# Attention stage of a two-layer trunk: the low parts of the weights of keys, values and queries on GpSimd, and taps 12 to 21 of the last two convolution chunks ahead of the blocks' additions

## Time and profile before

| | us |
|---|---|
| three runs | 1467.14, 1471.12, 1465.32 (median 1467.14) |
| profiled execution | 1472.86 |
| its span, first to last instruction | 1471.1 |
| PE busy | 1447.4 (98%) |
| VectorE busy | 1188.1 (81%) |
| ScalarE busy | 932.8 (63%) |
| GpSimd busy | 60.4 (4%), 70 instructions |
| line 990 (the taps), VectorE | 103.6, 240 instructions |
| line 961 (low parts of dense and expert weights), VectorE | 843.7, 369 instructions of 2.29 |

### The profile page before, as it was taken

The page is one execution under the profiler, slowest core; times in us unless marked ns, Lnnn a source line. Parts: engine busy times, 40 slices in busy tenths (PEclk is TensorE's granted clock), DMA queues, the critical chain, the costliest instruction groups (busy, mean ns, idle before and its releaser), DMA issues.

```text
span 1471.1 us, 18960 instructions
## 1 busy us (share of the span) xinstructions
PE 1447.4 (98%) x7380; PEld 1189.1 (81%) x7380; DVE 1188.1 (81%) x1109; ACT 932.8 (63%) x878; POOL 60.4 (4%) x70
## 2 busy tenths in 40 slices
PE   7999999999999999999999999999999999999998
PEld 6864999998765888888888888888888888888886
DVE  5995545447995788988898898888889888889887
ACT  4273343434373777777777777777777777777774
POOL 1042000000141000000000000000000000000000
PEclk9999999999999899999999999999999999999999
DMA  7750755532822799999999999999999999999993
GB/s 245 231 170 34 253 188 185 172 115 89 278 94 82 274 363 375 369 363 354 339 364 369 376 351 365 370 336 364 369 369 363 356 371 330 365 376 364 367 368 132
DMA packets 203853, 426.62 MB, mean 290 GB/s; under 512 B 7410, under 2 KB 48626, under 8 KB 203764
## 3 DMA queue, kind: packets, MB, share of 16 engines
q1 hardware_dynamic: 202448, 424.90, 80.6%
q10 hardware_dynamic: 1316, 0.49, 0.1%
HBM read 424.31 MB, written 1.05 MB: 289 GB/s over the span
## 4 chain that ended last, share of the span: by engine, by line
PE 87%; DVE 11%; issue 1%; ACT 1%; DMA 1%; ACTq 0%; POOL 0%; DVEq 0%
PE bank L1922 14%; PE bank L1924 14%; PE bank L1923 14%; PE bank L1944 7%; PE bank L1946 7%; PE bank L1945 7%; DVE arena L990 6%; PE bank L1826 3%; PE bank L1828 3%; PE bank L1827 3%; PE bank L1655 2%; PE bank L1456 2%; PE bank L1932 2%; PE bank L1843 1%; PE bank L1844 1%; PE bank L1845 1%
## 5 line engine op out<-in xcount | busy, mean ns | idle before, releaser
L961 DVE TENSOR_TENSOR w_split<-ring,w_split 128x2048 fp32r<-128x2048 f32 x369 | 843.7, 2290 | 192.6 <-ACT w_split L585 191.0
L585 ACT CAST w_split<-ring 128x2048 fp32r<-128x2048 f32 x369 | 706.0, 1914 | 295.6 <-PE bank L1924 161.6
L1922 PE MATMUL bank<-w_split,xe_hi 128*128 128x512 f32 x896 | 355.0, 396 | 0.0
L1924 PE MATMUL bank<-w_split,xe_lo 128*128 128x512 f32 x896 | 349.7, 390 | 0.0
L1923 PE MATMUL bank<-w_split,xe_hi 128*128 128x512 f32 x896 | 348.9, 389 | 0.0
L1924 PEld LDWEIGHTS bank<-w_split,xe_lo 128*128 128x128 f32 x896 | 168.2, 188 | 36.3
L1922 PEld LDWEIGHTS bank<-w_split,xe_hi 128*128 128x128 f32 x896 | 168.3, 188 | 34.9 <-DVE w_split L961 1.2
L1923 PEld LDWEIGHTS bank<-w_split,xe_hi 128*128 128x128 f32 x896 | 168.5, 188 | 33.2
L1944 PE MATMUL bank<-w_split,actT_hi 128*128 128x512 f32 x448 | 175.2, 391 | 0.0
L1946 PE MATMUL bank<-w_split,actT_lo 128*128 128x512 f32 x448 | 174.5, 389 | 0.0
L1945 PE MATMUL bank<-w_split,actT_hi 128*128 128x512 f32 x448 | 174.4, 389 | 0.0
(11 more groups left out here) (239 smaller groups left out, 1424.1 us busy)
## 6 DMA issues: line engine op xcount, KB each, us to landing
ring<-in_moe_w SPq DMA_DIRECT2D x336, 1024.0 KB, 5.8
ring<-in_dense_w SPq DMA_DIRECT2D x33, 1024.0 KB, 5.4
ring<-in_w_in SPq DMA_DIRECT2D x8, 1024.0 KB, 9.5
ring<-in_w_in SPq DMA_DIRECT2D x4, 2048.0 KB, 8.2
ring<-in_w_out SPq DMA_DIRECT2D x4, 2048.0 KB, 7.9
ring<-in_cmp_k_w SPq DMA_DIRECT2D x2, 2048.0 KB, 14.0
ring<-in_cmp_v_w SPq DMA_DIRECT2D x2, 2048.0 KB, 9.3
ring<-in_w_in SPq DMA_DIRECT2D x2, 1120.0 KB, 12.5
```

The lines of the kernel that those rows point to most:

```text
L585: nc.scalar.copy(split_part(0, t), raw(t)).then_inc(w_hi_ready, 1)
L961: V.tensor_tensor(split_part(1, t), raw(t), split_part(0, t).bitcast(F32), ALU.subtract).then_inc(w_lo_ready, 1)
L1922: T.matmul(dst, xe_hi[:, kk, own], hi[:, k, :], start=(kk == 0), stop=False)
L1924: last = T.matmul(dst, xe_lo[:, kk, own], hi[:, k, :], start=False, stop=(kk == KD - 1))
```

## The change

`z_low` moves from VectorE's list to GpSimd's, where it stands behind `norm(2 * l)` and ahead of `qk_deviations`, in the order (1,0), (1,1), (0,0), (0,1). Its arithmetic, buffers and semaphores stay. In VectorE's list the four calls go, and taps 12 to 21 of chunks 2 and 3 are done in one go in front of `blocks(0)`; they were spread before: tap 12 behind `square_sums_z(0)`, 13 to 15 ahead of `compressed_keys`, 16 around `maxima(5, 0)` and 17 to 21 ahead of `scaled_probs(4, 0)`. `conv_taps` now calls `next_tap(c)`, which keeps for every chunk its next tap and the count of its last step, and waits for that count. `group_means(0)` waits for 106 steps.

```diff
--- before.py
+++ after.py
@@ -375,7 +375,7 @@
         MEAN_BANK, VAR_BANK, DEV_BANK = (0, 1), (4, 6), (3, 1)
         ZDUP_BANK, HID_BANK, KC_BANK, CS_BANK = (6, 7), 2, 6, 7
         Q_BANK, K_BANK, CPT_BANK, O_BANK = (4, 0), (1, 3), (4, 6), (3, 0)
-        Q_TURN, K_TURN, CONV_COUNT = (2, 4), (1, 3), (94, 124)
+        Q_TURN, K_TURN, CONV_COUNT = (2, 4), (1, 3), (106, 124)
         S_BANK = ((7, 5), (4, 2), (1, 3), (6, 5), (2, 0), (1, 7))
         PT_BANK = ((0, 7), (4, 5), (4, 6), (5, 6), (5, 6), (0, 7))
         WO_BANK = ((4, 3), (2, 5))
@@ -529,7 +529,15 @@
                     nc.gpsimd.tensor_tensor(p3, p3, pscale[:, n, kv, 0:nh].unsqueeze(2).to_broadcast([P, nh, keys]),
                                             ALU.mult).then_inc(p_ready, 1)
 
+                def z_low(c, part):
+                    pl.wait_ge(z_hi_ready, 4 * l + 2 * (1 - c) + part + 1)
+                    nc.gpsimd.tensor_tensor(z_lo[part], view("win", l, 2 + c)[:, 4 * part:4 * part + 4, :],
+                                    z_hi[part].bitcast(F32), ALU.subtract).then_inc(z_lo_ready, 1)
+
                 norm(2 * l)
+                for c in (1, 0):
+                    for part in range(2):
+                        z_low(c, part)
                 qk_deviations(0)
                 qk_deviations(1)
                 compressed_deviations()
@@ -975,33 +983,34 @@
                     dv.wait_ge(sig_ready, CC * l + c + 1)
                     V.tensor_tensor(u[:, c, PAD:], bank[GLU_BANK[c]][:, 0:S], sig[:, c % 2, :], ALU.mult).then_inc(u_ready, 1)
 
+                tap_of, last_step = [0] * CC, [0] * CC
+
+                def next_tap(c):
+                    tap = tap_of[c]
+                    w = p_(l, "conv_w", c * TAPS + tap)
+                    if tap == 0:
+                        dv.wait_ge(u_ready, CC * l + c + 1)
+                        V.tensor_scalar(y[:, c, :], u[:, c, 0:S], w, p_(l, "conv_b", c), ALU.mult,
+                                        ALU.add).then_inc(conv_step, 1)
+                    else:
+                        dv.wait_ge(conv_step, last_step[c])
+                        V.scalar_tensor_tensor(out=y[:, c, :], in0=u[:, c, tap:tap + S], scalar=w,
+                                               in1=y[:, c, :], op0=ALU.mult, op1=ALU.add).then_inc(conv_step, 1)
+                    conv_n[0] += 1
+                    tap_of[c], last_step[c] = tap + 1, conv_n[0]
+
                 def conv_taps(c0, taps):
 
-                    if taps[0] == 0:
-                        dv.wait_ge(u_ready, CC * l + c0 + 2)
                     for tap in taps:
                         for c in (c0, c0 + 1):
-                            w = p_(l, "conv_w", c * TAPS + tap)
-                            if tap == 0:
-                                V.tensor_scalar(y[:, c, :], u[:, c, 0:S], w, p_(l, "conv_b", c), ALU.mult,
-                                                ALU.add).then_inc(conv_step, 1)
-                            else:
-                                dv.wait_ge(conv_step, conv_n[0] - 1)
-                                V.scalar_tensor_tensor(out=y[:, c, :], in0=u[:, c, tap:tap + S], scalar=w,
-                                                       in1=y[:, c, :], op0=ALU.mult,
-                                                       op1=ALU.add).then_inc(conv_step, 1)
-                            conv_n[0] += 1
+                            if tap_of[c] <= tap:
+                                next_tap(c)
 
                 def attention_low(i, h):
                     part = (slice(None), slice(4 * h, 4 * h + 4), slice(i * P, (i + 1) * P))
                     dv.wait_ge(aT_hi_ready, 4 * l + 2 * i + h + 1)
                     V.tensor_tensor(aT_lo[part], hT[part], aT_hi[part].bitcast(F32), ALU.subtract) \
                         .then_inc(aT_lo_ready, 1)
-
-                def z_low(c, part):
-                    dv.wait_ge(z_hi_ready, 4 * l + 2 * (1 - c) + part + 1)
-                    V.tensor_tensor(z_lo[part], view("win", l, 2 + c)[:, 4 * part:4 * part + 4, :],
-                                    z_hi[part].bitcast(F32), ALU.subtract).then_inc(z_lo_ready, 1)
 
                 def glu_low(c):
                     for half in range(2):
@@ -1147,9 +1156,7 @@
                 glu(0)
                 glu(1)
                 conv_taps(0, range(0, 2))
-                z_low(1, 0)
                 conv_taps(0, range(2, 6))
-                z_low(1, 1)
                 conv_taps(0, range(6, 7))
                 glu(2)
                 conv_taps(0, range(7, 9))
@@ -1170,8 +1177,6 @@
                 conv_taps(2, range(6, 7))
                 conv_taps(0, range(16, 17))
                 conv_taps(2, range(7, 8))
-                z_low(0, 0)
-                z_low(0, 1)
                 conv_taps(0, range(17, 18))
                 conv_taps(2, range(8, 9))
                 conv_taps(0, range(18, 19))
@@ -1181,23 +1186,20 @@
                 conv_taps(0, range(20, 21))
                 conv_taps(2, range(11, 12))
                 conv_taps(0, range(21, 22))
+                conv_taps(2, range(12, 22))
                 blocks(0)
                 blocks(1)
                 conv_taps(0, range(22, 23))
                 square_sums_z(0)
                 conv_taps(0, range(23, 24))
-                conv_taps(2, range(12, 13))
                 square_sums_z(1)
                 conv_taps(0, range(24, 25))
                 normalised_z(0)
                 conv_taps(0, range(25, 26))
                 normalised_z(1)
                 conv_taps(0, range(26, 27))
-                conv_taps(2, range(13, 14))
                 conv_taps(0, range(27, 28))
-                conv_taps(2, range(14, 15))
                 conv_taps(0, range(28, 29))
-                conv_taps(2, range(15, 16))
                 compressed_keys()
                 conv_taps(0, range(29, 30))
                 maxima(0, 0)
@@ -1227,9 +1229,7 @@
                 maxima(4, 1)
                 scaled_probs(3, 1)
                 maxima(5, 0)
-                conv_taps(2, range(16, 17))
                 maxima(5, 1)
-                conv_taps(2, range(17, 22))
                 scaled_probs(4, 0)
                 conv_taps(2, range(22, 24))
                 scaled_probs(4, 1)
```

## The result

The changed kernel took 1506.61 us (median of four, 1505.91 to 1512.78) beside 1469.13 before (four, 1465.32 to 1473.16): ratio 1.0272, 95% interval 1.0251 to 1.0293. It is slower by 37.5 us where 25.0 were forecast, and its time lies above the range (1477 to 1504). The runs of these two kernels fall near two values some 6 us apart, two and two before, three and one after, so that the lowest differ by 40.6, the highest by 39.6 and the medians by 37.5. The profiled execution has a span of 1505.2, 34.1 more than the one of before.

A forecast was written before the change was run, and what follows sets the result against it. The prediction took VectorE to bound the attention part, with TensorE nearly tight between blocks and compressed keys. +13.1 us a layer less 0.55 gave +12.5, 25.0 for two layers: 1492.1 us on the median, range 1477 to 1504.

The forecast's parts named there:

- Direction and the cause named: Whole kernel: slower, because GpSimd's subtractions lock VectorE out over whole instructions; chance 0.78 for this cause, 0.87 for slower.
- half of what was to show it: Signs: 4 us taps, two each in 31 to 41 and 54 to 63 us; the 20 taps end near 79.
- -8.8 and +7.9: VectorE ahead of the blocks, per layer: four low parts removed, -8.8 us; ten taps of two chunks moved there, +7.9.
- The lock-out: Each of four GpSimd subtractions per layer shuts VectorE out for 3.7 us, at least 3.16 and at most 4.16.
- At most half a microsecond of wait, and covered: TensorE's product of queries: wants the last low part at 62.3, done between 61.1 and 62.6; TensorE waits for blocks anyway.
- The prediction's own condition for TensorE becoming the bound: Late low parts make TensorE the bound only if GpSimd takes some 10 us for one; folded into the upper end.
- The blocks: 79.35 forecast: Blocks' start in layer 0: 66.05 - 8.8 + 7.9 - 0.6 + 4 x 3.7 = 79.35 us.
- The moved taps: Ten taps of two chunks: +7.9 us ahead of the blocks; behind them only 0.4 and 0.55 come back.
- The clock: compress() after TensorE's idle time runs at a lowered clock at first: 1.7 us charged per layer, lower end 0.
- One upper case: Forecast with half the upper clock loss, 2.7 us more: 17.0 a layer, 1501 us.
- TensorE's idle time ahead of compress(): Sign: TensorE idle 10 to 13 us ahead of compress(), put down to VectorE's blocks.
- Idle time ahead of scaled_probs(4, 0): Sign: VectorE idle about 4 us in front of scaled_probs(4, 0), put down to ScalarE.

The follow-up runs named there:

- e1: Changed kernel with taps 12 to 21 back in their old order, so only the low parts move to GpSimd: 1491.99 us beside 1467.66, ratio 1.0161.
- e3b: Changed kernel with two one-column memsets in VectorE's stream, 28 and 32 taps into it: 1498.81 us beside 1467.7, ratio 1.0196.
- e2: Kernel before with only the taps moved ahead of the blocks, low parts left on VectorE: 1483.13 us beside 1467.66, ratio 1.0104.
- e8: Changed kernel with 150 unread transposes ahead of the products of queries, keeping TensorE busy: 1507.73 us beside 1467.15, ratio 1.0278.
- e4_near_waits: Changed kernel with every tap waiting for the last step but one, as before, not its own chunk's last: 1508.98 us beside 1467.66, ratio 1.0268.
- e12_weighted_dve: Kernel before with four multiplications, weighted(4, 0) to weighted(5, 1), moved from GpSimd to VectorE: 1466.0 us beside 1466.95, ratio 0.9994.
- e10: Kernel before with only chunk 1's low parts on GpSimd and no tap moved: 1475.29 us beside 1467.15, ratio 1.0049.

## Why the prediction was wrong

- **Direction and the cause named, right; half of what was to show it, not there.** A lock-out over whole instructions makes GpSimd's help dearer than the 2.20 us it saves. Where GpSimd gets in, it is as told: two long taps in 31 to 41, of 4.8 us where 4 was said. The two long taps told for 54 to 63 are missing, and the taps ended at 73.5 and not near 79.
- **-8.8 and +7.9, right.** e1's and the changed kernel's streams differ by 26.20 - 18.30 = 7.90. The taps ended at 66.1 before and at 73.5 after, +7.4, and -8.8 + 7.9 + 2 x 4.33 - 0.39 is 7.4.
- **The lock-out, too small and outside the bounds.** 3.7 taken, 3.16 to 4.16 allowed, 4.33 measured; the instruction is 4.51 where 3.4 to 4.16 was given. The bound was four times the square's 1.04; the weighted multiplication beside it, 1.22, would have given 4.9. The Trainium skill (GPSIMD Engine Reference, § 3.1) has 4.497 us for a 2048-column addition, and the trace agrees with 4.51 for a subtraction. Worth 4 x 0.63 = 2.5 a layer.
- **"At most half a microsecond of wait, and covered": the step that failed.** TensorE waited 18.00 us for the third low part. The step took it that the engines change turns at any request. In the rows it rested on the earlier trace rows, VectorE had just done something other than a string of taps; no row had GpSimd ask amid one, and the kernel's longest was exactly where the queries' low parts would fall. The prediction's own condition for TensorE becoming the bound (some 10 us for one subtraction) was met with 23.4. compress() then started 20.6 us later where 11.8 were forecast.
- **The blocks: 79.35 forecast, 86.46 measured.** With the breaks of e3b they came at 81.42, which the forecast's sum gives with 4.33 for 3.7 (81.9). So 2.1 is the size of the lock-out and 5.0 the stream. The total follows: e3b +31.1 beside 25.0, inside the range, and the changed kernel about +40, outside it.
- **The moved taps, right in size, by another way.** They were counted as work ahead of the blocks. In fact they lengthen the stream that keeps GpSimd out, and the blocks then wait on a chain in which VectorE idles for 12.92. Either way it is 7.9 a layer.
- **The clock, wrong here.** 1.7 for compress() was somewhat low where compress() follows the pause: 2.1 in e2, 3.0 in e3b. In the changed kernel the pause sat before the product instead, compress() ran its 7.13 at full clock, and e8 shows that the slow product cost nothing. That this term stood in the sum at all brought it 3.4 us nearer to the result by luck.
- **One upper case is added up wrongly.** Half of the upper clock loss is 7.13 / 2 = 3.6, which is 1.9 more than the 1.7 charged and not 2.7; the case gives 16.2 a layer and 1499.5, not 1501. The forecast doesn't hang on it.
- **TensorE's idle time ahead of compress(), wrong.** It stands ahead of line 1481 and is put down to GpSimd.
- **Idle time ahead of scaled_probs(4, 0), right:** 4.50 by ScalarE, where about 4 was forecast; and at the compressed keys TensorE is late (2.08), as said.
- **The lock was right as far as it goes.** The Trainium skill (SBUF — State Buffer, § Who interferes with whom) tells of a lock held for a whole instruction, and the trace agrees for the first two subtractions (4.33 us of lock-out beside 4.51). Who gets the next turn was the question here.

## What to carry to other kernels

Before a long GpSimd instruction is put beside VectorE, look at what VectorE does when it will ask: behind ten or more two-input SBUF instructions in a row it waited here for the end of the string, whether that was 28 taps off (e1) or 48, and a reader of its result waited too. One memset of 0.06 us in the string let it in, so try that before giving the idea up; but count first, since even at once it took 4.33 us of VectorE for 2.20 of work saved, and no kernel here gained by it. A row that shows two engines taking turns shows it only for the neighbours that they had.

## What else the runs showed

- **A stream keeps GpSimd out**, with a step between 6 and 10 taps (above). The stream itself doesn't slow (0.397 us a tap with GpSimd's instruction open), so nothing is to be seen on VectorE's side; only GpSimd's duration tells.
- **The dense phase has two paces.** 1056 float32r matmuls of 256 columns ran at 117.8 ns each in some executions and 113.6 in others, 4.4 us over the phase, also with the same instruction order (the changed kernel 113.6, e4_near_waits 117.8; before 117.8, e12_weighted_dve 113.6), in all four at a granted clock of 1.00 in this phase. The weight loads of line 1828 carry the mark, in nanoseconds (min/median/max), the kernel before first and then the changed one:

```profile
L1828 PEld LDWEIGHTS bank<-hT_hi,w_split x352: 192/192/192, 151.3 to 324.9; 128*128 128x128 f32 x176
```

```profile
L1828 PEld LDWEIGHTS bank<-hT_hi,w_split x352: 187/188/189, 171.3 to 340.3; 128*128 128x128 f32 x176
```

  The three profiled executions at the slow pace (before, e4 and e10) are all of the longer runs of their kernels, so this may be most of the 6 us between the two values. Why an execution gets the one or the other stays open; it is larger than some effects that one would want to read from a single profile.
- **Four times the columns cost more than four times the lock-out**: 0.79 us at 128x512 (weighted), 4.33 at 128x2048 (the subtraction). GpSimd's own time doesn't say it as clearly: four times the square's 1.04 is 4.16 and four times the 1.22 of weighted is 4.9, and the subtraction took 4.51. They differ in operands as well, and this wasn't separated.
